# Even layer of a two-layer trunk: one sequence of weight groups, heads paired by parity, output norms and masks moved

## The chip, the cores and the metric

One core of one Trainium2 chip runs the whole program. The metric is the device time of one execution in microseconds (us); lower is better. TensorE is called PE, VectorE DVE, ScalarE ACT, GpSimd POOL and SyncE SP, as in the profile.

## The reference, cut to what matters

x is 512 tokens by 1024 features, float32. Layer 0 (the even layer) is a mixer of four gated DeltaNet heads and four differential-attention heads and then a gated MLP; layer 1 (the odd layer) is a chunk-band attention of 16 heads and another MLP.

```python
h = rmsnorm(x, even_norm_mix)
dn_qkv, dn_a, dn_b, dn_gate, fq, fk, fv = split_cols(h @ even_w_in, IN0_SPLITS)
dn_qkv = silu(causal_dwconv(dn_qkv, even_dn_conv))            # 4 taps
# gated_deltanet, per head: L = I + strict(beta * k k^T * decay); solve L [u|w] = [beta v | beta k exp(g)]
#   qk = tril(q k^T * decay); scan over chunks: v_new = u - w S; o = q_dec S + qk v_new; S = S*g_last + k_dec^T v_new
o_a = rmsnorm(o_a, even_dn_norm) * silu(dn_gate)
# diff_attention, per head: softmax(q1 k1^T) - lam * softmax(q2 k2^T), rotary q and k, block-causal mask
o_b = rmsnorm(o_b, even_diff_subln) * (1.0 - lam_init)
x = x + concatenate([o_a, o_b]) @ even_w_out
x = x + conv_gated_mlp(rmsnorm(x, ffn_norm[0]), ...)
x = x + chunk_band_attention(rmsnorm(x, odd_norm_mix) @ odd_w_qkv) @ odd_w_out
x = x + conv_gated_mlp(rmsnorm(x, ffn_norm[1]), ...)
out = rmsnorm(x, final_norm)
```

## The kernel before

**Layout.** Features lie on the 128 partitions and the 512 tokens along the free axis. Every large product is made of three matmuls of 128x512 in a split format: `mm3` (L619 to L621) multiplies head by head, tail by head and head by tail, where head is a value rounded to the fast format (`mh`, `wh`) and tail the remainder (`ml`, `wl`). The prediction calls three such matmuls a **group**. Eight groups over k make one 128-feature tile in one of four accumulators `acc`.

**Weights.** They come in units through two slots. SP loads 128x2048 floats into `raw[s]`, ACT rounds them into `wh[s]` (L373, `units_split_act`), DVE subtracts (L377, `units_split_dve`) into `wl[s]`. A slot can be split again only when PE has finished both tiles of the unit in it. In the even layer slot 0 holds q and k of a DeltaNet head and slot 1 its v and gate; for an attention head slot 0 holds q and k, slot 1 only v.

**Order.** Each engine has its program written out by hand, in order; semaphores tie them. Four PSUM tensors `R0` to `R3` serve all small products in a fixed order of jobs (`BANK`). Python generators interleave: PE walks a chain of small products and takes groups from `fill` between them; ACT and DVE walk their side and take pieces from `evac` (a convolution, a split, a SiLU) at fixed places.

**DeltaNet.** `dn_pair(p, ...)` does heads 2p and 2p+1 side by side. PE: sums of squares (L658), cumulative decays (`grow`, L720), norms spread over rows (`rk`, `rq`, L740), kk, qk, two transposes, a doubling series At, A2 ... U3, three rounds T, Y, X, then u, wT, a scan over four blocks, and at its end the output norm: square on ACT, sums on PE (`oc`), root, reciprocal, diagonal matrix, spread on PE (`ro`), and two DVE products. Before pair 0 PE has done four units (64 groups) in the opening. Two groups are taken after every step: pair 0 has 64 groups, pair 1 has 24. POOL applies the masks `triu` and `C_STRICT` to the decays before DVE uses them (L520, L523), and copies the gate (L517).

**Attention.** `attention("diff", i, ...)` runs in a hardware loop for heads 0 to 2 and once for head 3. For each of 8 score tiles DVE adds the mask and negates (L1662), ACT exponentiates (L1189); after two of them DVE normalises and combines (L1672 to L1682), PE transposes (L865), ACT copies, PE multiplies by v (L880). PE takes two groups after each of 8 steps and one after the later ones; then the next head's rotary products (L826), `stack` on ACT (L1092 to L1094) and key tails on POOL (L549), and the output norm of this head follow (L658, L1717, L895, L1221, L1723). DVE evacuates the next head's q, k, v after the last score tile.

**Output projections.** The last even head and the last odd pair take groups of the projection of the first three tiles over seven of the eight inputs; `out_rest` then does the eighth input of the three tiles, and after that all eight groups of the fourth tile. The next unit follows.

Of the kernel before, what the change touches and what calls it, by code (L numbers as in the profile page):

```python
# [30 lines left out]
P = 128  # L31
S = 512
# [15 lines left out]
ALPHA = 4  # L48
LINE = 40
# [11 lines left out]
C_ID, C_ONE, C_TRIU, C_STRICT, C_M16, C_M32, C_M64, C_M128, C_PERM = range(9)  # L61
C_COS, C_SIN, C_MASK = 9 * P, 9 * P + S, 9 * P + 2 * S
C_WIDTH = 9 * P + 3 * S


def constants():
# [26 lines left out]
_DN = [("sq_c", 0), ("grow", 1), ("gcol", 0), ("rk", 0), ("kk", 0), ("rq", 0), ("qk", 1), ("ktok", 0), ("vtok", 1),  # L93
# [13 lines left out]
class Bank:  # L107
# [5 lines left out]
    def phase(self, name, jobs, times, lead=()):  # L113

        for j in lead:
            self.at[dict(jobs)[j]] += 1
        self.base[name] = (list(self.at), jobs)
        for _, b in jobs:
            self.at[b] += times
        for j in lead:  # L120
            self.at[dict(jobs)[j]] -= 1
# [12 lines left out]
BANK.phase("dn", DN_JOBS, NH // 2)  # L134
BANK.phase("diff", DIFF_JOBS, NH, lead=("rot_q", "rot_k"))
# [5 lines left out]
BANK.phase("yt", XT_JOBS, 1)  # L141

# [15 lines left out]
def build(nc, T, out):  # L158

    ctx = ExitStack()  # L160
    with ctx:
# [90 lines left out]
        own = ("gC", "sqq", "sqk", "qh", "kh", "decT", "decN", "qd", "qkD", "N", "A", "At", "A2", "A2t", "U")  # L252
        d = [{}, {}]
        for n in ("gC", "sqq", "sqk", "qh", "kh", "decT", "decN", "qd"):
            for h in (0, 1):
                d[h][n] = sb(f"dn_{n}{h}", [P, S], F32, mix)[:, :]
# [1586 lines left out]
```

## Time and profile before

| | |
|---|---|
| three runs | 1481.82 us median (1476.59 to 1482.45) |
| profiled execution | 1482.28 us, span 1480.6 us |
| PE busy | 1415.0 us, 96% |
| DVE busy | 843.7 us, 57% |
| ACT busy | 617.9 us, 42% |
| granted PE clock, mean | 0.968 |
| PE share of the chain that ended last | 88% |

A granted clock of 1.00 is 2.4 GHz and 0.50 is 1.2 GHz. The mean of a stretch between these says how much of it ran at the lower level: at 0.95, a tenth of it. As half speed costs half of that time, (1 - clock) times the length of a stretch in which PE is busy is what the lower level cost there.

The even layer's mixer lies in the first 413 us; the opening ends at 74.9 us, pair 0 at 186.4, pair 1 at 273.8, the first attention head starts at 288.3.

### The profile page before, as it was taken

What the parts mean: (1) busy time and instruction counts of PE and PEld (TensorE: products, weight loads), DVE (VectorE), ACT (ScalarE), POOL (GpSimd) and SP (SyncE); (2) the same over time, 40 slices, a digit from 0 to 9 for tenths busy, and PEclk for the clock granted to TensorE, in tenths of its full rate; (3) what the DMA queues carried; (4) which work ended last, traced back from release to release, by engine and by line L of the source; (5) the groups of instructions that cost most, each with busy time, mean ns of one, the idle gap of its engine ahead of it and who ended that gap; (6) DMA issues with size and microseconds to landing.
All of it is one profiled execution on the core that took longest, in us unless ns stands there. A gap on an engine that the chain in (4) does not pass through costs nothing.

```text
span 1480.6 us, 19860 instructions
## 1 busy us (share of the span) xinstructions
PE 1415.0 (96%) x6775; PEld 1154.3 (78%) x6775; DVE 843.7 (57%) x1235; ACT 617.9 (42%) x865; POOL 180.9 (12%) x177
## 2 busy tenths in 40 slices
PE   5979999899989999999999999999999999999996
PEld 4769888677777888888888777777778888888875
DVE  5676665566664655346555566556556654355542
ACT  4423232355533454223334566556434452233342
POOL 1040042011232100000001221112130000000011
PEclk9979979899999999999999999999999999999997
DMA  7421101011334542343323323223233323433131
GB/s 202 130 57 29 44 15 44 0 43 57 114 86 112 161 124 64 107 114 101 86 71 96 106 62 96 65 62 97 56 89 85 100 84 87 127 85 108 58 89 57
DMA packets 218641, 124.80 MB, mean 84 GB/s; under 512 B 6047, under 2 KB 215434, under 8 KB 218340
## 3 DMA queue, kind: packets, MB, share of 16 engines
q1 hardware_dynamic: 213744, 112.54, 27.0%
q0 software_dynamic: 3664, 11.58, 2.9%
q8 instruction: 29, 0.48, 0.1%
q10 hardware_dynamic: 1188, 0.08, 0.1%
q14 instruction: 16, 0.13, 0.0%
HBM read 119.94 MB, written 9.48 MB: 87 GB/s over the span
## 4 chain that ended last, share of the span: by engine, by line
PE 88%; DVE 5%; ACT 3%; issue 2%; DMA 1%; POOL 0%; DVEq 0%; ACTq 0%; SPq 0%; POOLq 0%
PE acc L619 24%; PE acc L621 23%; PE acc L620 23%; PE R L720 4%; PE R L880 4%; PE R L865 1%; PE R L848 1%; ACT wh L373 1%; PE R L658 1%; PE R L849 1%; PE R L740 1%; DVE wl L377 1%; DVE cta L1368 1%; PE R L718 1%; DMA xin<-in_x 1%
## 5 line engine op out<-in xcount | busy, mean ns | idle before, releaser
L619 PE MATMUL acc<-mh,wh 128*128 128x512 f32 x1120 | 456.0, 407 | 9.7 <-DVE ml L1321 5.4
L621 PE MATMUL acc<-mh,wl 128*128 128x512 f32 x1120 | 440.7, 393 | 0.0
L620 PE MATMUL acc<-ml,wh 128*128 128x512 f32 x1120 | 440.7, 393 | 0.0
L377 DVE TENSOR_TENSOR wl<-raw,wh 128x2048 fp32r<-128x2048 f32 x116 | 251.8, 2171 | 137.1 <-ACT wh L373 137.1
L373 ACT ACTIVATE wh<-raw 128x2048 fp32r<-128x2048 f32 x116 | 210.1, 1811 | 151.0 <-PE acc L621 149.7
L619 PEld LDWEIGHTS acc<-mh,wh 128*128 128x128 f32 x1120 | 213.0, 190 | 58.3 <-issue 11.9
L621 PEld LDWEIGHTS acc<-mh,wl 128*128 128x128 f32 x1120 | 212.5, 190 | 46.4
L620 PEld LDWEIGHTS acc<-ml,wh 128*128 128x128 f32 x1120 | 213.2, 190 | 41.5 <-issue 2.6
L494 POOL TENSOR_TENSOR ssum<-ssum,sq 128x512 f32<-128x512 f32 x32 | 52.0, 1624 | 719.9 <-ACT sq L1012 719.3
L619 PE MATMUL acc<-ah,wh 128*128 128x512 f32 x352 | 137.7, 391 | 0.4 <-DVE wl L377 0.2
L620 PE MATMUL acc<-al,wh 128*128 128x512 f32 x352 | 137.0, 389 | 0.0
L621 PE MATMUL acc<-ah,wl 128*128 128x512 f32 x352 | 137.0, 389 | 0.0
L1764 DVE SCALAR_TENSOR_TENSOR cta<-cb,pv,cta 128x512 f32<-128x512 f32 x88 | 66.2, 752 | 74.8 <-ACT cta L1260 68.4
L1189 ACT ACTIVATE pr<-ns,nm 128x128 f32<-128x128 f32 (+3 forms) x96 | 53.8, 561 | 89.5 <-DVE nm L1662 66.6
L1260 ACT ACTIVATE cta<-cb,pv 128x512 f32<-128x512 f32 x44 | 35.9, 816 | 103.8 <-DVE cb L1757 103.6
L619 PEld LDWEIGHTS acc<-ah,wh 128*128 128x128 f32 x352 | 66.0, 188 | 16.5 <-issue 2.4
L621 PEld LDWEIGHTS acc<-ah,wl 128*128 128x128 f32 x352 | 66.1, 188 | 13.9
L620 PEld LDWEIGHTS acc<-al,wh 128*128 128x128 f32 x352 | 66.1, 188 | 13.3
L1662 DVE CUSTOM_DVE_ANT_0 ns<-R,gb 128x128 f32<-128x128 f32 (+1 forms) x64 | 30.7, 489 | 66.2 <-PE R L849 66.2
L1784 DVE TENSOR_TENSOR x<-x,acc 128x512 f32 (+1 forms) x32 | 22.0, 687 | 72.6 <-PE acc L621 72.3
L880 PE MATMUL R<-pT,av 128*64 128x128 f32 (+1 forms) x400 | 60.7, 282 | 0.1
L880 PEld LDWEIGHTS R<-pT,av 128*64 128x64 f32 (+1 forms) x400 | 44.2, 147 | 15.9 <-issue 13.2
(282 smaller groups left out, 1755.9 us busy)
## 6 DMA issues: line engine op xcount, KB each, us to landing
raw<-in_ffn_w_in SPq DMA_DIRECT2D x88, 512.0 KB, 5.0
raw<-in_even_w_in SPq DMA_DIRECT2D x24, 512.0 KB, 5.2
raw<-in_ffn_w_out SPq DMA_DIRECT2D x32, 384.0 KB, 4.0
raw<-in_ffn_w_out SPq DMA_DIRECT2D x32, 320.0 KB, 3.6
raw<-in_odd_w_qkv SPq DMA_DIRECT2D x16, 512.0 KB, 4.6
rel_bias_extended<-rel_bias_rows POOLq DMA_DIRECT2D x16, 320.0 KB, 4.1
raw<-in_even_w_out SPq DMA_DIRECT2D x8, 512.0 KB, 4.7
raw<-in_odd_w_qkv SPq DMA_DIRECT2D x16, 256.0 KB, 3.1
```

The costliest lines, as they stand in the source:

```text
L373: nc.scalar.activation(wh[s][:, 0:n], raw[s][:, 0:n], ACT.Copy).then_inc(sem(f"w_head{s}"), 1)
L377: nc.vector.tensor_tensor(wl[s][:, 0:n], raw[s][:, 0:n], wh[s][:, 0:n].bitcast(F32), ALU.subtract).then_inc(sem(f"w_tail{s}"), 1)
L494: pool.tensor_tensor(ssum[:, :], ssum[:, :], sq[s][:, :], ALU.add).then_inc(sem("ssum"), 1)
L619: nc.tensor.matmul(o, ah_, bh_, start=first, stop=False)
L620: nc.tensor.matmul(o, ah_, bl_, start=False, stop=False)
L621: return nc.tensor.matmul(o, al_, bh_, start=False, stop=last)
L720: last = nc.tensor.matmul(r[:, t], lhs, triu if b is triu else b[:, t], start=True, stop=True)
L880: last = nc.tensor.matmul(dst, av[:, k, vc], pT[y % 2][:, k * P:(k + 1) * P], start=(k == 0), stop=(k == b))
L1189: A(pr[t % 2][:, 0:w], ns[t % 2][:, 0:w], ACT.Exp, bias=nm[:, t:t + 1], scale=-1.0, accum_out=rs[:, t:t + 1]).then_inc(sem("exp_" + ph), 1)
L1260: A(cta[s][:, :], cb[s][:, ALPHA - 2:ALPHA - 2 + S], ACT.Identity, bias=pv[:, bass.ds(j + (PV_CB + JF * layer), 1)], scale=pv[:, bass.ds(j ...
L1662: free(V.tensor_tensor_reduce(out=ns[t % 2][:, 0:w], in0=r[:, 0:w], in1=bias, scale=-1.0, scalar=3e38, op0=ALU.add, op1=ALU.min, accum_out ...
L1764: V.scalar_tensor_tensor(out=cta[s][:, :], in0=cb[s][:, o:o + S], scalar=pv[:, bass.ds(j + (w0 + JF * tap), 1)], in1=cta[s][:, :], op0=ALU ...
```

## The change

Four edits. (1) Weight groups of the even layer come in one sequence that PE takes from throughout: `give(fill, n)` takes n groups, `upto(fill, n)` takes until n are taken. Slot 0 holds even heads, slot 1 odd heads: q and k of head 0 and of head 1, then v and gate of head 0 and of head 1, and so on. Only the first two units (32 groups) come before pair 0. (2) The output norm of a pair is moved into the next pair (`post_sums`, `post_rows`, `post_roots`, `post_inverse`, `post_out`), that of an attention head into the next head (`diff_rows`, `diff_gain`, `diff_scale`, `diff_round`, `diff_tail`). (3) The masks of the decays are dropped; the strict triangle is in the masks of N, and POOL masks qkD afterwards. (4) The attention heads are written out instead of looped; the output projections take all four tiles as filler and `out_rest` is gone, in the odd layer too. All matrix products stay.

```diff
 # SP: units
+            for p in (0, 1):
+                for h in (0, 1):
+                    load(h, 2 * p, pair(h, w0, c + C_Q, c + C_K))
+                for h in (0, 1):
+                    load(h, 2 * p + 1, pair(h, w0, c + C_V, c + C_GATE))
...
 # PE: DeltaNet pair
                 for h in (0, 1):
                     pe.wait_ge(sem(f"sqk{h}"), p + 1)
                     token_sums(r, 0, d[h]["sqq"])
                     done(token_sums(r, NB, d[h]["sqk"]), ph, f"sq_c{h}", 0)
+                if p:
+                    post_sums(p - 1)
                 # grow, gcol
+                give(fill, 4)
+                spread(p, "rk", "sqk", "dk", p)
+                if p:
+                    post_rows(p - 1)
+                give(fill, 4)
+                step(4, "kk", "kh", "kh", ["rk"])
+                spread(p, "rq", "sqq", "dq", p)
+                give(fill, 4)
+                step(4, "qk", "kh", "qh", ["rq"])
+                step(4, "ktok", "kh", None)
+                two, one_ = (2, 1) if p == 0 else (1, 1)
+                step(two, "At", "A", None, need=[("A_E", 4 * p + 1)])
...
+                for w, e, g in (("16", "E32", (1, two, 1)), ("32", "E64", (two, 1, two)), ("64", "E128", (1, two, 1))):
...
 # PE: attention head
+            def diff_head(i, fill):
+                for t in range(12):
+                    if t < 8:
+                        score(ph, t, 0, t % 2, t // 2, i)
+                    if t == 0 and i == 0:
+                        post_rows(1)
+                    if t == 1:
+                        values(ph, 0, UNIT["diff"] + i)
+                    if t == 2 and i:
+                        diff_rows(i - 1)
+                    give(fill, 2 if t < 4 else 1)
+                    if t == 7 and i < NH - 1:
+                        rope_products(i + 1)
+                    # t = 3, 5, 7, 9: transposes; t = 4, 6, 8, 10: product with v
...
+            dn_pair(0, fill)
+            upto(fill, 68)
+            dn_pair(1, fill)
+            upto(fill, 120 + AHEAD)          # AHEAD = 8
+            post_sums(1)
+            for i in range(NH):
+                diff_head(i, fill)
+                if i < NH - 1:
+                    upto(fill, 120 + 24 * (i + 1) + AHEAD)
+                else:
+                    give(fill, 4)
+                diff_sums(i)
+            give(fill, 100)
+            diff_rows(NH - 1)
+            run(out_terms(out0, ((), (7,)), heads_wait, 1))
+            for s in (0, 1):
+                run(features(s, out0 + 1, (oh, ol)))
...
-            attention("odd", NPAIR - 1, out_terms(UNIT["out1"], range(KD - 1), KD - 1, pairs_wait))
-            out_rest(UNIT["out1"], KD - 1, pairs_wait)
+            odd_pair(NPAIR - 1, out_terms(out1, (range(KD - 1),), pairs_wait, 2))
+            run(out_terms(out1, ((), (KD - 1,)), pairs_wait, 2))
+            for s in (0, 1):
+                run(features(s, out1 + 1, (oh, ol)))
 # ACT: attention head
+                    if t < 8:
+                        read(act, ph, f"s{t}", 0)
+                        if t >= 2:
+                            act.wait_ge(sem("pn_diff"), 4 * i + t // 2)
+                        probabilities("diff", i, t, (t // 2 + 1) * P)
+                    if t == 2 and i:
+                        diff_gain(i - 1)
+                    if t == 4 and i:
+                        diff_round(i - 1)          # oh of the head before
+                    if t in (5, 6) and i in (1, 2):
+                        k = 2 * (i - 1) + t - 5
+                        A(oh[:, k, :], om[:, k, :], ACT.Copy).then_inc(sem("oc_head"), 1)
+                    # t odd: copy of the transposes
+                    if t == 8 and i < NH - 1:
+                        units_split_act(act, 0, UNIT["diff"] + i + 2)
...
 # DVE: attention head
+                for t in range(10):
+                    # mask and negate s_t; at t = 2, 4, 6, 8 normalise and combine
+                    if t == 1 and i == 0:
+                        post_out(1)
+                    if t == 2 and i:
+                        diff_scale(i - 1)
+                    if t == 4 and i:
+                        diff_tail(i - 1)           # waits for o_head from ACT
+                    if t in (5, 6) and i in (1, 2):
+                        dve.wait_ge(sem("oc_head"), k + 1)
+                        V.tensor_tensor(ol[:, k, :], om[:, k, :], oh[:, k, :].bitcast(F32), ALU.subtract)
+                    if t == 5 and i == NH - 1:
+                        rest_split_dve(dve, 0)
+                    if i < NH - 1:
+                        if t in (5, 6):
+                            rotated_evac(i + 1, t - 5)
+                        if t == 8:
+                            rope(i + 1)
+                        if t == 9:
+                            units_split_dve(dve, 0, UNIT["diff"] + i + 2)
+                # then osb, query_tails, value_evac, units_split_dve(1), reciprocal, diagonal
...
 # DVE: opening
+            first = qk_evac(0)
+            for _ in range(4): next(first, 0)      # q0, k0
+            # abT copy
+            for _ in range(2): next(first, 0)      # split of slot 0
+            # chain of small operations on a, b (as before), waiting for ab_e from ACT
+            for _ in first: pass                   # q1, k1, split of slot 1
```

## Rows read from the trace of the kernel before

**Rows 1.** The page, busy times and granted clock in 40 slices.

```profile
PE 1415.0 (96%) x6775; PEld 1154.3 (78%) x6775; DVE 843.7 (57%) x1235; ACT 617.9 (42%) x865; POOL 180.9 (12%) x177
...
PEclk9979979899999999999999999999999999999997
```

**Rows 2.** Waits of PE: for whom, total us, times, longest.

```profile
PE R L720 <- DVE dn_decT L1447: 7.6, 1, 7.6
PE R L848 <- POOL kl L549: 6.8, 4, 4.6
PE R L895 <- DVE osd L1717: 5.5, 4, 1.4
```

**Rows 3.** Stretches of the even mixer: length, busy per engine, granted clock, DMA.

```profile
74.90:86.30 11.40, 3.81 (x33) 3.72 (x31) 8.76 (x12) 5.76 (x7) 0.61 (x1) 0.63 0.37 92
86.30:186.40 100.10, 98.91 (x612) 86.77 (x612) 69.04 (x111) 26.31 (x41) 18.80 (x14) 0.96 0.15 38
186.40:199.70 13.30, 12.00 (x55) 9.97 (x55) 8.41 (x16) 7.12 (x10) 2.29 (x2) 0.66 0.16 40
199.70:273.80 74.10, 72.46 (x491) 65.04 (x492) 46.01 (x77) 17.45 (x29) 22.08 (x18) 0.95 0.09 22
273.80:288.30 14.50, 8.87 (x27) 4.59 (x26) 8.07 (x14) 5.39 (x10) 1.25 (x1) 0.69 0.00 1
288.30:319.60 31.30, 29.20 (x137) 23.21 (x137) 19.20 (x46) 17.08 (x35) 5.46 (x5) 0.93 0.11 28
319.60:350.90 31.30, 29.13 (x136) 22.62 (x136) 21.30 (x49) 18.53 (x36) 5.69 (x4) 0.95 0.19 52
350.90:382.30 31.40, 29.15 (x137) 22.60 (x137) 21.38 (x49) 18.65 (x37) 5.71 (x4) 0.94 0.24 67
382.30:413.40 31.10, 26.61 (x123) 21.09 (x123) 15.51 (x42) 16.21 (x33) 4.25 (x6) 0.88 0.31 106
413.40:423.70 10.30, 10.28 (x33) 8.32 (x34) 6.74 (x5) 4.18 (x5) 3.80 (x2) 0.72 0.17 48
```

**Rows 4.** Chain that ended last, pair 0: start, length, what.

```profile
114.06 1.78 PE R L720 x16
117.24 1.78 PE R L720 x16
```

**Rows 5.** DVE in order of time in the opening: start, length, operation.

```profile
58.60 0.18 DVE L1611 TENSOR_TENSOR abz<-R,rcol 128x32 f32<-128x32 f32 x1
...
63.74 0.69 DVE L1356 TENSOR_TENSOR cb<-acc,rstd 128x512 f32<-128x512 f32 x1
...
68.67 2.32 DVE L1368 SCALAR_TENSOR_TENSOR cta<-cb,pv,cta 128x512 f32<-128x512 f32 x3
74.69 2.29 DVE L377 TENSOR_TENSOR wl<-raw,wh 128x2048 fp32r<-128x2048 f32 x1 [3.69 <-ACT wh L373]
...
86.24 0.42 DVE L1447 COPY dn_decT<-gall 128x512 f32<-128x512 f32 x1
```

**Rows 6.** Groups of DVE and ACT, each shape apart, attention head from 319.6 us.

```profile
L377 DVE TENSOR_TENSOR wl<-raw,wh 128x2048 fp32r<-128x2048 f32 x1 | 2.3, 2283 | 0.0
L1662 DVE CUSTOM_DVE_ANT_0 ns<-R,cst 128x512 f32<-128x512 f32 x2 | 1.4, 691 | 1.6 <-PE R L849 1.5
L1682 DVE SCALAR_TENSOR_TENSOR pn<-pr,rr,pn 128x512 f32<-128x512 f32 x1 | 0.8, 752 | 0.0
L1430 DVE TENSOR_TENSOR aq<-R,cst 128x512 f32<-128x512 f32 x1 | 0.7, 691 | 0.7 <-PE R L826 0.7
...
L1189 ACT ACTIVATE pr<-ns,nm 128x512 f32<-128x512 f32 x2 | 1.4, 725 | 2.4 <-DVE pn L1682 2.4
L1204 ACT ACTIVATE oh<-om x1 | 0.6, 615 | 0.0
```

**Rows 7.** ACT and DVE in order of time behind the odd projection's eighth input.

```profile
1064.65 1.92 ACT L373 ACTIVATE wh<-raw 128x2048 fp32r<-128x2048 f32 x1 [2.56 <-PE acc L621]
...
1066.60 2.29 DVE L377 TENSOR_TENSOR wl<-raw,wh 128x2048 fp32r<-128x2048 f32 x1 [1.14 <-ACT wh L373]
```

More of the change, by code:

```diff
@@ L48 @@
 ALPHA = 4
+AHEAD = 8
 LINE = 40
@@ L133 @@
 BANK.phase("norm0", NORM_JOBS[1:], 1)
-BANK.phase("dn", DN_JOBS, NH // 2)
-BANK.phase("diff", DIFF_JOBS, NH, lead=("rot_q", "rot_k"))
+for _p in (0, 1):
+    BANK.phase(f"dn{_p}", DN_JOBS[_p], 1)
+BANK.phase("dn2", DN_POST, 1)
+BANK.phase("rope", ROPE_JOBS, 1)
+for _i in range(NH):
+    BANK.phase(f"diff{_i}", [j for j in DIFF_JOBS if (_i or j[0] != "ro") and (_i < NH - 1 or j not in ROPE_JOBS)], 1)
+BANK.phase(f"diff{NH}", DIFF_POST, 1)
 BANK.phase("norm1", NORM_JOBS, 1)
@@ L540, in _ @@
                             .then_inc(sem(f"A_E{h}"), 1)
+                for h in (0, 1):
+                    e = d[h]
+                    read(pool, ph, f"qk{h}", 0)
+                    pool.tensor_tensor(blk(e["qkD"]), blk(e["qkD"]), rows(triu), ALU.mult).then_inc(sem(f"qkD{h}"), 1)
             def key_tails(n):
@@ L857, in attention @@
-                    run(fill, 2 if t < 8 else 1)
-                    z = (t - 3) // 2 if diff and (t - 3) % 2 == 0 else t - 2 if not diff else -1
-                    if 0 <= z < per:
-                        b = z if diff else items[z][1]
-                        pe.wait_ge(sem("pn_" + ph), per * i + z + 1)
-                        r = job(ph, f"t{z}", i)
-                        for k in range(b + 1):
-                            last = nc.tensor.transpose(r[:, k * P:(k + 1) * P], pn[z % 2][:, k * P:(k + 1) * P], ident)
-                        done(last, ph, f"t{z}", i)
@@ L1144, in dn_pair @@
-                next(evac, 0)
+                copy_out("At", "At")
+                copy_out("A2", "A2", 1)
+                copy_out("A4", "A4", 2)
+                copy_out("A8", "A8")
+                copy_out("T16", "T", 0 if p else 1)
+                copy_out("T32", "T", 0 if p else 2)
+                copy_out("T64", "T")
+                copy_out("wT", "wT", 1 if p else 3)
+                if p:
+                    stack("diff", 0)
                 for h in (0, 1):
-                    r = full(act, "dn", f"o{h}", p)
-                    A(d[h]["sqo"], r[:, :], ACT.Square).then_inc(sem(f"sqo_dn{h}"), 1)
+                    read(act, ph, f"o{h}", 0)
+                    A(d[h]["sqo"], d[h]["os"], ACT.Square).then_inc(sem(f"sqo_dn{h}"), 1)
@@ L1159, in _ @@
+            first = qk_evac(0)
+            for _ in range(3):
+                next(first, 0)
             act.wait_ge(sem("ab_in"), 1)
@@ L1441, in beta, with dn_pair, piece @@
+            def dn_pair(p, evac, pieces):
+                ph = f"dn{p}"
                 def beta(h):
                     return ball[:, 2 * p + h, :]
+                def piece(at):
+                    for _ in range(pieces.get(at, 0)):
+                        next(evac, 0)
                 for h in (0, 1):
@@ L1646, in attention @@
                 for t in range(8 + 2):
-                    if t == 9 and diff and more:
-                        next(evac, 0)
-                        rope(i + 1)
                     if t < 8:
@@ L1794, in mlp @@
                         x_tiles(3, g0 + 3, False)
-            with dve.Fori(0, NH - 1) as i:
-                attention("diff", i, NH, 0, att_evac("diff", i + 1, i + (UNIT["diff"] + 1)))
-            rest_split_dve(dve, 0)
-            attention("diff", NH - 1, NH, 0, iter(()), more=False)
+            for i in range(NH):
+                diff_head(i)
+            diff_scale(NH - 1)
+            diff_tail(NH - 1)
             out_proj(UNIT["out0"], 1)
```

1011 lines of the change are left out of this document (514 added, 497 removed), and 7 rows, old and new, of the table _DN.

## The prediction, before the changed kernel ran

> **What bounds the kernel now.** I read the page first: PE is busy 96% of the span [rows 1]. Every product stays in the change, so the time can move only by PE's idle time and by the time PE spends at the lower clock. The slices show the clock below full in the first third only, in the even mixer. The waits name three holes there [rows 2]: 7.6 us before pair 0, 6.8 us for key tails (4.6 of it before attention head 0), 5.5 us for the output norm of the four heads. Third view: the mixer in stretches [rows 3]. In each I add idle time (length minus PE busy) and clock loss, (1 - clock) x length:
>
> - opening's end, 74.9: 11.4 us long; the sums in it are about 3.6 us at full clock, so 7.8 us are lost
> - pair 0: 1.2 + 4.0 = 5.2
> - end of pair 0, 186.4: 1.3 + 4.5 = 5.8
> - pair 1: 1.6 + 3.7 = 5.3
> - end of pair 1, 273.8: 5.6 + 4.5, less what overlaps; the work in it is 5.4 us at full clock (three pieces of 1.8), so 9.1
> - four attention heads: 2.1, 2.2, 2.3, 4.5 idle and 2.2, 1.6, 1.9, 3.7 clock: 20.5
>
> That is some 54 us, 3.6% of the span, all that this change can win. Where the clock falls is plain: in stretches that are full of matmuls it is 0.93 to 0.96, in those with one-column sums and waits 0.63 to 0.72 [rows 3].
>
> **The change part by part.** The sum is made against the profiled execution, 1482.3 us (span 1480.6, 1.7 us around it); the median of the three runs is 0.5 us lower.
>
> A step of the DeltaNet chain is 1.78 us for both heads, and from step to step 3.18 us with two groups between [rows 4]; so a group is 0.70 us.
>
> *Opening, +2.2.* Pair 0 now starts after 32 groups, at 53.0 us instead of 74.9 (22 us of groups earlier). But its sums need k of head 1, and on DVE that convolution now stands behind the small chain on a and b, which takes 63.74 - 58.60 = 5.14 us [rows 5]. Its input comes from PE at about 47.6, so q1 starts at 52.7. A convolution is 3.6 us, two end at 60.0. From the end of such a convolution (68.67 + 2.32 = 71.0) through the squares, ACT's split and DVE's split it was 6.0 us (74.69 + 2.29) [rows 5], then 0.6 for the copies that release `grow`: 66.6. PE waits or sums from 53.0 to 66.6, 13.6 us against 11.4. The clock after it is taken as before. Bounds: -1 if the small chain hides under the tile, +5 if ACT's table changes fall on the path.
>
> *Pair 0, +0.8.* 68 groups instead of 64, which is only work moved in; four of them stand at each early step, one or two later. POOL's four masks of the decays and two gate copies go and two masks of qkD come, all before their users are due; PE waited for none of them [rows 2], so I count nothing. One new place: ACT does k's SiLU, two squares and a split before the T64 copy, 0.8 us late. Bounds 0 to +3.
>
> *Pair 0 to pair 1, 0.* The output norm no longer holds PE, but the first sums of pair 1 need the convolution of k3, which DVE does only after the last scan block: 3.6 us, SiLU and squares 1.9, ACT's split 1.9, DVE's split 2.3, copies 0.6. That is 10.3 us after the last scan operand, and PE has 5.4 us of sums and one group in it. It was 5.8 lost; it is 5 to 7. Bounds -3 to +3.
>
> *Pair 1, -2.7.* It has 52 groups instead of 24, so the steps that stood bare are covered; DVE's two evacuations of 0.7 and a piece of up to 1.95 us fit in 2.5 us per step on average. What stays is the clock after the sums. Bounds -4 to +2.
>
> *Pair 1 to head 0, -4.2.* Eight groups (5.6 us) cover rope, `stack` (six ACT copies, 3.6) and the square. But `post_rows(1)` stands right after the first score, while DVE must do a split and wait for a root before the diagonal: about 2.1 us idle, 0.3 before, and 2.5 of clock. 4.9 instead of 9.1. Bounds -7 to 0.
>
> *Heads.* This is the dear place. A head is 27.3 us of PE work (31.3 less 2.1 and 1.9). PE now takes one group, not two, after scores 4 to 7, has 8 groups after the head, and these need slot 0's split, which DVE does at t = 9, behind `rope` (four operations of 0.69, 2.8 us) [rows 6]. DVE and ACT are in order and hand to each other. For heads 1 and 2, from score 4 (8.6 us into the head): negate 0.64; combine 1.25; exponential 0.8 and rounding 0.6 on ACT, for which `diff_tail` waits; tail 0.69; negate 0.64; exponential 0.8 and `oh` copy 0.62, for which `ol` waits; `ol` 0.69; rotated q 0.68; negate 0.77; combine 1.5; exponential 0.75 and `oh` 0.62; `ol` 0.69; rotated k 0.68; negate 0.77; exponential 0.8; combine 1.6; rope 2.8; split 2.28. The widest forms are in [rows 6] (0.691, 0.752, 0.725, 0.615, 2.283), the narrower ones are from the same view. Sum 20.7 us. PE's own work from score 4 to those 8 groups is 12.3 us (four scores 2.3, eight groups 5.6, rotary products 1.8, transposes and products with v 2.6). So PE waits 8.4 us per head, in three or four places: before the product with v of block 1, before the rotary product of k, before the 8 groups. With an estimated 1.2 of clock that is 9.6 each, against 3.8 and 4.2: +11.2. Head 0 has neither `diff_tail` nor `ol`: 2.2 before the 8 groups and 0.8 of clock, against 4.3: -1.3. Head 3 has no rope but the tail and the rest split: PE waits 3.7; its final chain (square, root, diagonal, spread, scale, round, tail) stays bare, 4.5 idle and 3.0 clock; 11.2 against 8.2: +3.0. Together **+12.9**. Bounds -8 (DVE keeps up, no clock lost) to +24 (clock low through them). I take the sum, as it is made of measured durations in the order of the code.
>
> *Loop written out, 0.* The heads' instructions are issued once instead of from a loop; no row shows PE waiting for instructions in either form. Bounds -2 (registers at the loop's ends) to +3. SP's loads are as many and as large, and no PE wait here is for a load.
>
> *Projections, +7.2.* `out_rest` did eight groups (5.6 us) of the fourth tile behind slot 0's last input, and they covered slot 0's next split. Now only two groups follow. ACT's split starts after slot 0's last matmul, DVE's ends 68.89 - 64.65 = 4.24 us later [rows 7]. PE has 1.4 us: 2.9 idle, 0.8 clock, +3.7 in the odd layer, in which nothing else changes. In the even layer the clock is at 0.72 there [rows 3], the two groups take longer, so 2.0 idle and 1.5 clock, +3.5. Bounds +4 to +11.
>
> Sum: 2.2 + 0.8 + 0 - 2.7 - 4.2 + 12.9 + 0 + 7.2 = +16.2. 1482.3 + 16.2 = 1498.5; against the median, **1498 us**.
>
> The Trainium skill ("TensorE: Matmul & The Clock Gate", section "A second HAM failure mode: psum-queue depth-cycling") says that frequent short idles between groups of matmuls can make the clock swing between its two levels, so that the loss is more than the idles. By it, heads 1 and 2 and the pair with thinner filler would run partly at 1.2 GHz. That is the rival "low clock" below; the rows so far show it only around the sums and the long waits.
>
> **The rivals.** *Low clock, 1510.* If the waits inside heads 1 to 3 hold the clock at 0.75 over 90 us, as 0.63 to 0.72 stand in the short stretches [rows 3], that costs up to 22 us where I have 3.5, half of it inside waits: +12. Against: pair 1 with bare steps stayed at 0.95.
>
> *DVE keeps up, 1481.* DVE is busy 57% [rows 1] and 21.3 of 31.3 us in a head [rows 3]. If ACT's copies come before they are needed, heads 1 to 3 wait 2.3 each before the 8 groups. Heads 1 and 2: 6.2 against 8.0, -1.8; head 0 -1.3; head 3 nothing: -3.1 in place of +12.9, so 1482.
>
> *Faster, 1465.* One mechanism: the 8 groups ahead also outlast the split, because DVE reaches `rope` by PE's time, and PE never stops long enough to lose its clock in head 0 to 3. Then the 12.3 us of heads 0 to 2 go, the end of pair 1 gives 9, pair 1 gives 3, the projections cost 5 and the opening 2: -17. It decides by whether `wl` of slot 0 is written before PE has done the product with v of block 3. For it: all three holes of [rows 2] are addressed. Against: the sum of 20.7.
>
> *The norm isn't off the path.* If `diff_rows` still waits for the diagonal as L895 does, 1.4 to 1.5 us per head [rows 2], three heads keep 4.3 us more: 1503.
>
> **How the numbers follow.** Forecast 0.50 (own range 1489 to 1507); low clock 0.10; keeps up 0.17; faster 0.20; the norm 0.03. Within 0.5% of 1481.8 (1474.4 to 1489.2) is no change that a measurement tells. Slower: nearly all of forecast, low clock and norm, and little of keeps up, 0.59; same 0.20; faster 0.21. The range 1466 to 1511 leaves out one in ten on either side.
>
> **What would show it.** Right: in each of heads 1 and 2, PE waits over 5 us in total, on ACT's copy of transposes, DVE's rotated k, and `wl`; a head lasts about 36 us; a wait of 2 to 3 us on `wl` behind both projections; `grow` of pair 0 at 66 to 67 us. Wrong: heads of 28 to 30 us, or no wait on `wl` at about 1065 us plus the shift.

## The result, and the profile after

| | before | after |
|---|---|---|
| median of 12 runs, us (lowest to highest) | 1481.1 (1475.9 to 1482.5) | 1486.4 (1484.0 to 1489.7) |
| profiled execution, us | 1482.3 | 1484.7 |
| its span, us; mean granted clock | 1480.6; 0.968 | 1482.9; 0.972 |

After to before is 1.0042 (95% interval 1.003 to 1.0054). The change costs 6.2 us by that ratio, 5.3 by the medians and 2.4 between the two profiled executions, by which the stages below are compared. 16 were forecast. The profiled execution of the kernel before is 1.2 us above its median and that of the changed kernel 1.7 below, so the stages show the change some 3 us kinder than the medians; no profile says in which stage.

The page of the changed kernel, busy times and granted clock, against [rows 1]:

```profile
PE 1407.8 (95%) x6775; PEld 1149.7 (78%) x6775; DVE 857.3 (58%) x1251; ACT 615.3 (41%) x864; POOL 176.4 (12%) x169
...
PEclk9899899998989999999999999999999999999998
```

PE has as many matmuls. The low slices are still in the first third (and the last slice): four in both, at 8 now, where three stood at 7. PE's waits, against [rows 2] (for whom, total us, times, longest):

```profile
...
PE R L660 <- ACT dn_sqk L1142: 9.3, 2, 7.3
PE R L857 <- DVE nm L1776: 7.4, 3, 4.1
PE acc L621 <- DVE wl L384: 5.5, 4, 3.0
...
PE R L920 <- ACT pT L1279: 5.3, 3, 2.5
```

Of the three rows of [rows 2] the key tails are gone; of the diagonals of the attention heads' output norms only the last head's is left (1.3 us), and of the wait before `grow` 1.0 us. In their place stand the waits that the forecast named: for the squares before pair 0, for a rotary product behind a DVE step (L857), for ACT's copy of transposes (L920) and for the second step's weights (L621).

The stretches, against [rows 3]: opening's end, pair 0, its end, pair 1, its end, heads 0 to 3, projection:

```profile
52.90:66.30 13.40, 5.15 (x31) 4.98 (x30) 9.34 (x16) 6.66 (x9) 0.00 (x0) 0.65 0.00 1
66.30:165.30 99.00, 97.98 (x622) 86.85 (x622) 70.26 (x112) 25.39 (x38) 18.04 (x12) 0.98 0.17 43
165.30:176.70 11.40, 9.36 (x53) 9.14 (x52) 8.71 (x18) 6.59 (x10) 0.00 (x0) 0.69 0.12 29
176.70:267.90 91.20, 91.20 (x583) 80.48 (x584) 62.54 (x98) 22.28 (x34) 21.61 (x16) 0.96 0.08 21
267.90:275.70 7.80, 7.80 (x45) 6.67 (x44) 5.59 (x9) 6.05 (x10) 3.36 (x2) 1.00 0.52 132
275.70:310.20 34.50, 30.53 (x140) 22.31 (x139) 25.26 (x53) 18.17 (x35) 6.19 (x4) 0.95 0.18 47
310.20:346.70 36.50, 29.86 (x138) 22.82 (x137) 23.82 (x50) 19.03 (x37) 5.13 (x4) 0.91 0.16 44
346.70:382.10 35.40, 30.08 (x138) 23.04 (x137) 23.76 (x50) 19.03 (x37) 7.91 (x9) 0.90 0.26 68
382.10:413.65 31.55, 24.07 (x125) 18.55 (x125) 14.71 (x42) 14.10 (x31) 0.00 (x0) 0.97 0.26 91
413.65:425.90 12.25, 10.42 (x27) 7.77 (x28) 8.75 (x8) 6.79 (x8) 3.79 (x2) 0.65 0.31 85
```

PE shows as busy for all of pair 1, yet pair 1 isn't free of losses: ends of matmuls are modelled, so a short wait between two of them hides in the busy time. A better measure of a stage is its length less its PE work at the full clock, the work counted by the distances of matmuls that wait for nothing (0.227 us for one of a group's three, 0.11 for a 128-column one of a DeltaNet step). The rest is lost, to waits or the clock. By it, in us:

| stage | lost before | lost after | difference | forecast |
|---|---|---|---|---|
| opening's end | 8.2 | 10.3 | +2.2 | +2.2 |
| pair 0 | 7.3 | 3.6 | -3.8 | +0.8 |
| end of pair 0 | 5.5 | 5.5 | -0.1 | 0 |
| pair 1 | 8.8 | 3.1 | -5.7 | -2.7 |
| end of pair 1 and head 0 | 14.0 | 7.7 | -6.3 | -5.5 |
| heads 1 and 2 | 10.8 | 20.0 | +9.2 | +11.2 |
| head 3 | 9.0 | 9.1 | +0.2 | +3.0 |
| even projection | 2.8 | 6.2 | +3.4 | +3.5 |
| odd projection | 0.7 | 3.4 | +2.7 | +3.7 |
| start of the last MLP | 3.2 | 5.7 | +2.5 | 0 |
| program's end | 18.8 | 16.3 | -2.5 | 0 |
| all between (430 to 1060, 1110 to 1440 us) | 33.7 | 34.4 | +0.7 | 0 |

The rows add up to +2.5 as rounded; the profiled spans differ by 2.3. The start of the last MLP and the program's end, for which nothing was forecast, cancel each other.

Head 1 shows the chain that the forecast summed. Three answers, in order of time: PE, then DVE, then ACT (start, length, what, idle before):

```profile
324.56 0.71 PE L920 MATMUL R<-pT,av 128*128 128x128 f32 x4 [2.45 <-ACT pT L1279]
331.55 1.19 PE L857 MATMUL R<-qr,cst 128*128 128x512 f32 x1 [4.14 <-DVE nm L1776]
```

```profile
321.81 0.69 DVE L1843 TENSOR_TENSOR ol<-osb,oh 128x512 fp32r<-128x512 f32 x1 [1.36 <-ACT oh L1299]
...
324.27 0.69 DVE L1816 TENSOR_TENSOR ol<-om,oh 128x512 fp32r<-128x512 f32 x1 [1.29 <-ACT oh L1271]
...
329.50 0.69 DVE L1816 TENSOR_TENSOR ol<-om,oh 128x512 fp32r<-128x512 f32 x1 [1.46 <-ACT oh L1271]
330.11 0.68 DVE L1506 SCALAR_TENSOR_TENSOR qr<-acc,rstd 128x512 f32<-128x512 f32 x1
330.71 0.68 DVE L1776 CUSTOM_DVE_ANT_0 ns<-R,cst 128x512 f32<-128x512 f32 x1
```

```profile
323.01 0.61 ACT L1250 ACTIVATE pr<-ns,nm 128x384 f32<-128x384 f32 x1 [1.23 <-DVE nm L1776]
...
323.62 0.61 ACT L1271 ACTIVATE oh<-om 128x512 fp32r<-128x512 f32 x1
324.14 0.36 ACT L1279 ACTIVATE pT<-R 128x256 f32<-128x256 f32 x1
...
328.14 0.72 ACT L1250 ACTIVATE pr<-ns,nm 128x512 f32<-128x512 f32 x1 [3.64 <-DVE pn L1806]
```

Three times DVE idles 1.3 to 1.5 us for a rounding on ACT (`oh`) that stands behind an exponential, which waited for DVE. PE's second rotary product (`rot_k`) waits for what comes last in this line: it goes into the PSUM tensor that holds score 7 (`R1`), and DVE reads that score at 330.71, behind the third `ol` and `qr`. Hence the releaser `nm`, that is L1776, and not `qr`.

### The profile page after: what moved, and what is told of

Read it like the earlier page. It is cut to its first block, busy times and chain, and to the rows that moved or that the text cites. A ratio compares the mean times of both kernels' runs of the same rounds, so it can differ in the third digit from the quotient of the medians.

```text
span 1482.9 us, 19623 instructions
## 1 busy us (share of the span) xinstructions
PE 1407.8 (95%) x6775; PEld 1149.7 (78%) x6775; DVE 857.3 (58%) x1251; ACT 615.3 (41%) x864; POOL 176.4 (12%) x169
## 4 chain that ended last, share of the span: by engine, by line
PE 87%; DVE 6%; ACT 3%; issue 2%; DMA 1%; SPq 0%; ACTq 0%; DVEq 0%; POOL 0%; POOLq 0%
PE acc L621 24%; PE acc L623 23%; PE acc L622 23%; PE R L754 5%; PE R L950 3%; PE R L882 1%; PE R L868 1%; PE R L660 1%; DVE wl L384 1%; ACT wh L380 1%; PE R L869 1%; PE R L742 1%; PE R L752 1%; DMA xin<-in_x 1%; DVE cta L1462 1%
## 5 line engine op out<-in xcount | busy, mean ns | idle before, releaser
L621 PE MATMUL acc<-mh,wh 128*128 128x512 f32 x1120 | 458.7, 410 | 10.3 <-DVE ml L1412 5.4
L384 DVE TENSOR_TENSOR wl<-raw,wh 128x2048 fp32r<-128x2048 f32 (+1 forms) x108 | 233.5, 2162 | 118.1 <-ACT wh L380 118.0
L621 PEld LDWEIGHTS acc<-mh,wh 128*128 128x128 f32 x1120 | 213.1, 190 | 58.8 <-issue 12.2
L621 PE MATMUL acc<-ah,wh 128*128 128x512 f32 x352 | 137.7, 391 | 0.4 <-DVE wl L384 0.2
L621 PEld LDWEIGHTS acc<-ah,wh 128*128 128x128 f32 x352 | 66.0, 188 | 16.5 <-issue 2.4
L623 PEld LDWEIGHTS acc<-ah,wl 128*128 128x128 f32 x352 | 66.1, 188 | 13.9
L1776 DVE CUSTOM_DVE_ANT_0 ns<-R,gb 128x128 f32<-128x128 f32 (+1 forms) x64 | 30.7, 489 | 65.3 <-PE R L869 65.3
L621 PE MATMUL acc<-oh,wh 128*128 128x512 f32 x128 | 53.7, 419 | 10.5 <-DVE wl L384 4.8
L1357 ACT ACTIVATE ah<-pd 128x512 f32 x44 | 27.8, 632 | 69.7 <-DVE pd L1922 69.7
```

The lines of the kernel that those rows point to most:

```text
L384: nc.vector.tensor_tensor(wl[s][:, 0:n], raw[s][:, 0:n], wh[s][:, 0:n].bitcast(F32), ALU.subtract).then_inc(sem(f"w_tail{s}"), 1)
L621: nc.tensor.matmul(o, ah_, bh_, start=first, stop=False)
L623: return nc.tensor.matmul(o, al_, bh_, start=False, stop=last)
L1776: free(V.tensor_tensor_reduce(out=ns[t % 2][:, 0:w], in0=R[t % 2][:, 0:w], in1=bias, scale=-1.0, scalar=3e38, op0=ALU.add, op1=ALU.min, ac ...
```

## The experiments

Each ran beside the kernel before, and its ratio is to that kernel; edits are to the changed kernel except in `masks_only`. Most ratios rest on twelve executions of the experiment; `combo` has four, `combo_rows` five, `bare_pair1` six and `open_order` seven. Each has one profile. Waits that the expectations quote are from issue to issue, 0.1 to 0.2 us more than the view of waits shows.

**masks_only.** The kernel before with edit (3) alone.

```diff
-    put(C_M16, row // 16 == col // 16)
+    put(C_M16, (row // 16 == col // 16) & (col < row))
...
-                    pool.tensor_tensor(blk(d[h]["decT"]), blk(d[h]["decT"]), rows(triu), ALU.mult)
...
+                    pool.tensor_tensor(blk(e["qkD"]), blk(e["qkD"]), rows(triu), ALU.mult)
```

> The kernel before, with only the edit of the masks: GpSimd no longer multiplies the decays by the triangle ahead of the inverse; the lower triangle is folded into the masks of N, and qk times decay is masked behind them. Theory (GpSimd's masks of the decays were waited for by nobody for long): pair 0 and pair 1 keep their lengths within 0.7 us each, ratio 0.999 to 1.0. Rival (the masks stood on the path into the inverse, and their leaving it explains part of the 3.2 us and 5.5 us by which the pairs got better): each pair shorter by 1.5 us or more, ratio 0.998 or less.

Measured: ratio 0.9998 (0.9985 to 1.0011). Pair 0 and pair 1, against [rows 3]:

```profile
86.30:186.70 100.40, 99.00 (x612) 86.80 (x612) 68.91 (x111) 26.75 (x42) 15.97 (x12) 0.96 0.15 37
199.30:274.20 74.90, 73.04 (x494) 65.31 (x494) 45.34 (x77) 17.98 (x30) 19.53 (x16) 0.95 0.09 22
```

POOL is 2.5 to 2.8 us less busy in each. The bounds of these windows are not quite those of [rows 3]; from `grow` to the pair's output norm, pair 0 is 0.2 us shorter and pair 1 0.1 us longer than before. So that edit is worth nothing by itself, as the forecast had it. (The 3.2 and 5.5 us in the expectation are a first reading of the pairs' gains; the table above has 3.8 and 5.7.)

**bare_pair1.** The filler of pair 1 away from the steps of the inverse.

```diff
-                step(4, "ktok", "kh", None)
-
-                two, one_ = (2, 1) if p == 0 else (1, 1)
+                step(22 if p else 4, "ktok", "kh", None)
+
+                two, one_ = (2, 1) if p == 0 else (0, 0)
...
-                for w, e, g in (("16", "E32", (1, two, 1)), ("32", "E64", (two, 1, two)), ("64", "E128", (1, two, 1))):
+                for w, e, g in (("16", "E32", (one_, two, one_)), ("32", "E64", (two, one_, two)), ("64", "E128", (one_, two, one_))):
...
+                two = two or 1
```

> The changed kernel, with the filler of pair 1 taken in bulk: 22 groups of matmuls run behind the transposes of k, and none between the 18 steps of the inverse (from At to X64), which in the changed kernel have one group each. Everything else, and the sum of groups, is as it is. My prediction priced the filler's gain in pair 1 at 2.7 us, that is the one wait over 0.2 us that was seen per step; the traces show 5.5 us between the two kernels. Theory (the group also hides the short waits, below 0.2 us, that each bare step has for ScalarE's or VectorE's copy of the step before): pair 1 grows by 5 us or more, and its length, 91.2 us, to over 96; each bare step starts a full copy (0.6 us or more) late, so that 18 steps could cost up to 11 us; ratio 1.008 to 1.012. Rival (the gain of pair 1 came from the bulk of groups ahead, or from the masks that left VectorE's queue): pair 1 grows by 3 us or less, ratio under 1.006.

Measured: ratio 1.0058 (1.0038 to 1.0078). Pair 0, then pair 1:

```profile
66.80:167.40 100.60, 99.64 (x622) 88.21 (x622) 70.19 (x111) 25.35 (x38) 18.05 (x12) 0.96 0.16 43
178.90:273.70 94.80, 93.92 (x583) 81.45 (x583) 58.94 (x98) 22.61 (x34) 20.71 (x16) 0.95 0.07 20
```

Pair 1 took 94.8 us in place of 91.0 (taken, here and in the table, between the matmuls that open the stages, up to 0.2 us from the windows' bounds): 3.8, between theory (5 or more) and rival (3 or less); the ratio, under 1.006, is the rival's. Of the 3.8 us 1.5 are waits over 0.2 us (from issue to issue), 1.0 the clock, the rest (1.3) short waits. And pair 0, whose code is the same, took 1.7 us more, all clock (0.96 for 0.98): a pair's length differs by that much from one profile to another. This profile is also the slowest of its six executions, so the 1.0 us of clock may be no work of the edit. The group beside each step is then worth 2.8 us in waits, and 3.8 with the clock: about what the forecast gave it, and not the 11 that fully bare steps could cost. The remaining 1.9 to 2.9 of pair 1's 5.7 this run leaves unexplained.

**heads_ol.** Two roundings of DeltaNet outputs to the front of heads 1 and 2, on ACT and on DVE.

```diff
-                    if t in (5, 6) and i in (1, 2):
-                        k = 2 * (i - 1) + t - 5
+                    if t in (1, 2) and i in (1, 2):
+                        k = 2 * (i - 1) + t - 1
```

> The changed kernel, with one step moved: the two roundings of a DeltaNet head's output (ScalarE's copy and VectorE's difference, two of each in attention heads 1 and 2) stand at scores 1 and 2 of the head and no longer at scores 5 and 6. Theory (after score 4 ScalarE and VectorE take turns on one chain, up to VectorE's split at the head's end; PE waits for that chain): two ScalarE copies of 0.63 us and two VectorE differences of 0.6 to 0.7 us leave the chain. Heads 1 and 2 fall by about 2.5 us each, from 36.5 and 35.4 us to about 34 and 33, and the wait of 4.29 us at 326.8 us to under 2.5; time -5 us, ratio 1.001. Rival A (VectorE's total work in the head is the limit, wherever its steps stand): under 1 us each, ratio 1.004. Rival B (TensorE's low clock sets these heads): no change either, and the granted clock of the two windows stays at 0.91.

Measured: ratio 0.9996 (0.9985 to 1.0007), 6.8 us less than the changed kernel; all that it had lost. Heads 0 to 3:

```profile
275.00:309.50 34.50, 30.54 (x141) 22.39 (x140) 25.25 (x53) 18.13 (x35) 6.20 (x4) 0.95 0.18 47
309.50:341.00 31.50, 27.82 (x139) 21.02 (x138) 23.42 (x50) 19.16 (x37) 6.20 (x4) 1.00 0.18 51
341.00:372.50 31.50, 27.84 (x139) 21.02 (x138) 23.40 (x50) 19.15 (x37) 8.88 (x9) 1.00 0.29 76
372.50:406.00 33.50, 26.46 (x123) 19.88 (x123) 14.75 (x42) 14.33 (x31) 0.00 (x0) 0.87 0.25 86
```

Head 1 fell by 5.0 us, head 2 by 3.9: the chain theory holds, rival A falls, and the size was too small by half, for a reason that the column of the granted clock shows (the third from the end): it went from 0.91 to 1.00. Of head 1's 5.0 us, 2.6 are waits (from issue to issue), as expected; the other 2.4 are clock that had fallen behind them. So rival B was half right: the clock did cost, but it wasn't a cause of its own. That is no accident of one profile: in all five profiles in which both roundings stand late, heads 1 and 2 take 36.5 and 35.4 us (to 0.2), and in all four in which both stand early, the clock is 1.00 in both heads. Head 3 gave 2.0 us back (31.5 to 33.5, clock 0.97 to 0.87) with its code unchanged.

**ol_one.** Only the first of the two moves (`if t in (1, 6)`).

> Half of heads_ol: in heads 1 and 2 only the first of the two roundings moves, from score 5 to score 1; the second stays at score 6. heads_ol took 5.0 us from head 1, of it 2.6 us of TensorE's waits and 6.8 us at the low clock, which at half speed are 2.4 us more. It leaves open whether the clock's part goes in step with the waits, or at once. Theory (the clock falls behind the long wait of 4.29 us, which one rounding less shortens by 1.3 us to about 3.0, like head 2's wait of 2.97 in the changed kernel, behind which the clock fell as well): heads 1 and 2 keep a low clock of 6.8 us each and shorten by about 1.3 us each, to 35.2 and 34.1; ratio 1.002. Rival (a wait of 3 us is short enough): the low clock goes with half of the move, both heads take 32 to 33 us, ratio 1.000.

Measured: ratio 1.0025 (1.0011 to 1.0039). Heads 1 and 2:

```profile
314.80:348.40 33.60, 28.97 (x138) 22.31 (x138) 23.65 (x50) 19.03 (x37) 5.13 (x4) 0.95 0.18 48
348.40:382.00 33.60, 28.94 (x139) 22.59 (x138) 23.63 (x50) 19.03 (x37) 7.83 (x9) 0.95 0.28 74
```

Both at 33.6, neither theory's 35.2 nor wholly the rival's. In head 1 the longest wait went from 4.1 to 2.8 us and the clock from 0.91 to 0.95: its part shrinks by degrees, here in step with the waits. The heads gained 4.7 us, but the ratio moved by only 2.5: in this profile, the slowest of its twelve executions, pair 0 is 1.7 us longer than in the changed kernel and head 0 1.0 us, with the same code and a lower clock.

**heads_both.** `heads_ol`, and ACT's rounding of the head before from score 4 to behind the transposes' copy at score 3.

```diff
-                    if t == 4 and i:
-                        diff_round(i - 1)
...
+                    if t == 3 and i:
+                        diff_round(i - 1)
```

> The kernel of heads_ol (the roundings of the DeltaNet outputs at scores 1 and 2 of heads 1 and 2), with one more step moved: ScalarE rounds the attention head before (the copy to oh) behind its copy of the first transposes at score 3, no longer behind the exponential of score 4. Theory (the chain of ScalarE and VectorE from score 4 on): in heads_ol VectorE waits 1.36 us for that copy of 0.62 us before it can subtract score 5's bias, so heads 1, 2 and 3 fall by 0.6 to 1.3 us each and the time by 2 to 4 us against heads_ol, to a ratio of 0.997 to 0.998. Rival (TensorE's waits of 0.86 and 1.87 us for the copies of the transposed probabilities are what these heads wait for now, and the copy now stands just ahead of them): no gain, 0.9996 or worse.

Measured: ratio 0.9978 (0.9964 to 0.9992). Heads 1 and 2:

```profile
311.20:341.20 30.00, 27.78 (x137) 20.95 (x138) 23.34 (x50) 19.15 (x37) 6.19 (x4) 1.00 0.20 53
341.20:371.30 30.10, 27.86 (x139) 21.01 (x138) 23.33 (x50) 19.15 (x37) 8.89 (x9) 1.00 0.31 80
```

They had 31.5 us each in `heads_ol`: 1.4 to 1.5 less, a little more than the 0.6 to 1.3 that the chain theory gave, while the total fell by 2.7 us, inside its 2 to 4.

**odd_hold.** The odd projection's fourth tile: five of its seven early inputs held back.

```diff
+                        if (s, t) == (1, 1):
+                            heads = [k for k in heads if k not in held]
+                            if n == len(parts) - 1:
+                                heads = list(late) + heads
...
+            odd_pair(NPAIR - 1, out_terms(out1, (range(KD - 1),), pairs_wait, 2, held=(2, 3, 4, 5, 6)))
+            run(out_terms(out1, ((), (KD - 1,)), pairs_wait, 2, late=(2, 3, 4, 5, 6)))
```

> The changed kernel, with the groups of the odd projection's second step put otherwise: of its fourth tile only the parts of heads 0 and 1 run beside the last pair of heads, those of heads 2 to 6 follow after the eighth head. So seven groups of matmuls (4.9 us), not two (1.4 us), lie between the end of the first step and the matmul that needs the split of the weights that this end sets free. Theory (that split, 4.2 us on ScalarE and VectorE one behind the other, is what TensorE waits for): the wait of 3.14 us at 1069 us is gone, and the time falls by 3 us, to a ratio of 1.002 against the kernel before; by 6 us (1.000) if the low clock at 1101 us hangs on that wait. Rival (the wait only moves, since the first five groups now sit in the chain of the last pair of heads less): the pair takes up to 3 us longer, time unchanged at 1.004.

Measured: ratio 1.0031 (1.0018 to 1.0045). PE at the second step, first in the changed kernel, then in this one:

```profile
1072.52 0.50 PE L621 MATMUL acc<-oh,wh 128*128 128x512 f32 x1 [2.97 <-DVE wl L384]
```

```profile
1067.26 0.39 PE L623 MATMUL acc<-oh,wl 128*128 128x512 f32 x1
1067.49 0.39 PE L621 MATMUL acc<-oh,wh 128*128 128x512 f32 x1
```

The wait of 2.97 us is gone, and matmuls follow each other by 0.23 us; behind it the kernel's lead on the changed one is 3.3 us larger than ahead of it. The total shows 1.6 us, which the two intervals leave anywhere from -1 to 4. The low clock at the start of the last MLP stayed (0.77 over 15 us, where before has 1.00), so it doesn't hang on that wait. That stretch in the changed kernel, then in the kernel before:

```profile
1095.00:1110.00 15.00, 12.31 (x45) 9.48 (x44) 6.93 (x6) 5.40 (x7) 4.29 (x3) 0.77 0.25 70
```

```profile
1093.00:1108.00 15.00, 12.29 (x55) 9.18 (x55) 8.28 (x8) 5.43 (x8) 4.30 (x3) 1.00 0.25 70
```

PE waits there twice for the same DVE step, 2.0 us at the longest, in both kernels. Nine of the ten profiles with the changed projections have this low stretch in full and neither of the two with the old ones has it; why the clock falls behind these waits in the one and not in the other stays open.

**both_hold.** The same in the even projection (3 to 6 held).

> odd_hold, with the even projection held in the same way: of its fourth tile only heads 0 to 2 run ahead, 3 to 6 follow the eighth head, so that TensorE has six groups (4.2 us) and no longer two beside the split of the second step's weights. My price of the even projection was 3.5 us (the wait and nothing else); the trace of the changed kernel shows a wait of 1.94 us at 418.5 us and a low clock there. Theory (the wait goes, and the four groups that are taken from head 3 were in its waits' cover only in part): 1.5 to 3 us less than odd_hold, a ratio of 1.001 to 1.002. Rival (the groups held were hiding head 3's last chain, whose waits of 1.43 and 3.14 us grow by as much): no change against odd_hold, 1.003.

Measured: ratio 0.9998 (0.9984 to 1.0012), 4.9 us less than `odd_hold`, more than expected. Of that 1.8 lie at the start of the last MLP, where the clock over 15 us is 0.89 and not 0.77; no run shows this to be the edit's work. Head 3 and what follows:

```profile
383.30:413.70 30.40, 22.02 (x113) 16.21 (x112) 14.74 (x42) 14.10 (x31) 0.00 (x0) 0.93 0.28 94
413.70:426.00 12.30, 12.15 (x46) 9.64 (x47) 8.82 (x8) 6.96 (x8) 3.81 (x2) 0.88 0.31 84
```

The wait for `wl` went from 1.8 to 0.2 us and the clock behind it from 0.65 to 0.88: 46 matmuls begin in the second stretch, 27 in the changed kernel. Head 3, with four groups (2.7 us) fewer, is only 1.1 us shorter (30.4 for 31.55). Of the 1.6 us that came back 0.9 are waits in the view of waits (a new one of 0.7 for ACT's square, and 1.5 for 1.3 at the diagonal); the rest goes with the lower clock (0.93 for 0.97). The rival is right in kind and outweighed.

**open_order.** DVE's convolutions of head 1 around the small chain: q's ahead of it, k's between its halves.

```diff
-            for _ in range(2):
+            for _ in range(4):
                 next(first, 0)
...
+            for _ in range(2):
+                next(first, 0)
             dve.wait_ge(sem("ab_e"), 5)
```

> The changed kernel, with VectorE's order in the opening turned: q's convolution of head 1 stands ahead of the small chain on a and b, and k's convolution between the two halves of that chain; the rest as it is. Theory (grow of pair 0 waits for VectorE's convolutions of head 1, which stand behind a chain of 5.1 us, three of them idle): pair 0 starts at about 63.2 us and not at 66.4, time -3 us, ratio 1.002. Rival (the same chain then ends later and holds ScalarE's table changes, so that the squares come no sooner): pair 0 starts at 65.5 us or later, ratio 1.004.

Measured: ratio 1.003 (1.0017 to 1.0043). PE from the first sums to `grow`, in the changed kernel and in this one:

```profile
52.64 0.95 PE L660 MATMUL R<-cst,dn_sqq 128*128 128x1 f32 x8
...
61.76 1.87 PE L660 MATMUL R<-cst,dn_sqq 128*128 128x1 f32 x8 [7.29 <-ACT dn_sqk L1142]
...
66.37 1.01 PE L754 MATMUL R<-cst,dn_decT 128*128 128x128 f32 x3 [1.03 <-DVE dn_decT L1578]
```

```profile
54.92 0.95 PE L660 MATMUL R<-cst,dn_sqq 128*128 128x1 f32 x8
...
60.64 1.87 PE L660 MATMUL R<-cst,dn_sqq 128*128 128x1 f32 x8 [3.89 <-ACT dn_sqk L1142]
...
65.31 2.07 PE L754 MATMUL R<-cst,dn_decT 128*128 128x128 f32 x8 [1.09 <-DVE dn_decT L1578]
```

From first sum to `grow` it is 10.4 us where it was 13.7: 3.3 less, as the theory has it. By the clock of the trace `grow` is at 65.3, since this run reached its first sum 2.3 us later. In the seven profiles whose opening is that of the changed kernel the sum stands between 51.3 and 53.8 us, and here PE's first matmul itself was 1.1 us late, so a bound on an absolute time was a poor test; the distance between two marks is the good one. That the turned order itself delays the first sum isn't excluded: `combo` and `combo_rows`, which have it, reach it at 53.7 and 51.9. The total (1.7 us less) is inside the intervals.

**combo.** `heads_both`, `both_hold` and `open_order` together.

> The edits of heads_both, both_hold and open_order together. Theory (each wait is paid by itself): the gains add up, 6.6 us for the first move in the heads, 2 to 4 for the second, 1.6 for the odd projection, 1.5 to 3 for the even one, 3 for the opening: 1471 to 1474 us on the median before of 1479.8, a ratio of 0.994 to 0.996, faster than either kernel. Rival (TensorE's low clock takes back part, since it comes behind the first wait that is left wherever that stands): the ratio stays at 0.998 or above.

Measured: 1464.6 us against 1480.6, ratio 0.9905 (0.9886 to 0.9924): 20.3 us less than the changed kernel, where the expected ratios meant 12 to 15. The three edits by themselves measured 9.5, 6.5 and 1.8, in sum 17.8, from which 20.3 is not clear by the intervals. Heads 1 and 2 take 30.1 us each, and from 403 us on the clock stays full up to the start of the last MLP, where the changed kernel had low stretches at 422 and 453 us. The rival isn't borne out: the clock took nothing back.

**combo_rows.** `combo`, and the spread of the last pair's norm one score later.

```diff
-                    if t == 0 and i == 0:
+                    if t == 1 and i == 0:
                         post_rows(1)
```

> The kernel combo, with the spread of the last pair's output norms moved in head 0 from behind score 0 to behind score 1, ahead of the transposes of v; the rest as it is. TensorE waits 1.90 us there for VectorE's diagonal, and then 1.25 us for the PSUM tile of the transposes, which VectorE frees late. Theory (score 1 and its operands are ready, so they cover part of the first wait): head 0 falls from 34.5 to 33.5 us or less, time -1 us, ratio 0.990. Rival (the second wait grows by what the first loses, since VectorE's evacuation follows from the diagonal and the norm it sends): head 0 unchanged, 34.5 us, ratio 0.9905. Should the clock fall no longer in head 0, 1.7 us come on top.

Measured: 1456.2 us against 1479.0, ratio 0.9844 (0.9823 to 0.9865), the fastest of all. The two waits of head 0 in the changed kernel, then head 0 in `combo`, then here:

```profile
PE R L742 <- DVE dn_A L1550: 1.7, 1, 1.7
PE R L876 <- DVE dn_A L1559: 1.1, 1, 1.1
```

```profile
273.60:308.10 34.50, 30.50 (x141) 22.40 (x140) 25.23 (x53) 18.13 (x35) 6.19 (x4) 0.95 0.18 47
```

```profile
271.40:301.60 30.20, 28.92 (x140) 21.28 (x140) 25.18 (x53) 17.98 (x35) 6.19 (x4) 1.00 0.21 53
```

One line moved by one score took 4.3 us off, where the theory had 1, and 2.7 with the clock. Both waits went, 2.6 us from issue to issue, and with them 1.7 us of clock ((1 - 0.95) x 34.5). Head 0 accounts for 4.3 us. The ratio moved by 9, on four and five executions; between the two profiles it is 5.6, of which 2.2 is a head 0 that starts earlier behind the same code, and behind head 0 the kernel is 0.9 us slower.

## Why the prediction was wrong

The sign came out, and so did the mechanisms in the opening, the attention heads and the projections; the size was 10 us too large by the ratio. The measured 1486 us lies below the forecast's own range (1489 to 1507), in the band that the prediction called "no change" and gave 0.20. The step that failed is the price of the two pairs. By the steps:

- *Opening, +2.2*: measured +2.2, `grow` at 66.37 for 66.6. `open_order` shows the cause named, DVE's convolution behind the small chain.
- *Pair 0, +0.8*: measured -3.8. **This term and the next failed.** I took the clock behind the sums "as before" and saw no wait worth removing. The waits over 0.2 us fell by 0.9 us (six became three), the clock's part by 2.2 (0.96 to 0.98, [rows 3]); 1.7 of that is what the clock does by itself from profile to profile: `bare_pair1` has it back with the same code, and of ten profiles with this pair 0 seven take 99.3 to 99.7 us from `grow` to the next sums and three 100.8 to 101.3. The masks had no part.
- *Pair 1, -2.7*: measured -5.7. I priced idle time and left the busy time alone; but a chain without filler also loses short waits between matmuls that the busy time swallows. `bare_pair1` puts 2.8 on the filler, 1.3 of it such short waits, and 1.0 more with the clock; 1.9 to 2.9 of the 5.7 it doesn't show, and their cause stays open.
- *Pair 1 to head 0 and head 0, -5.5*: measured -6.3. The wait at `post_rows(1)` is there (1.7 for 2.1 us).
- *Heads 1 and 2, +11.2*: measured +9.2; 36.5 and 35.4 us for "about 36". Right in kind: `heads_ol` and `heads_both` take links out of the chain and get their time back. The split between waits and clock was off. The forecast had 8.4 of waits and 1.2 of clock per head; head 1 had 6.5 of waits (rotary product 4.1, transposes 2.4) and 3.3 of clock ((1 - 0.91) x 36.5, a part of it inside the waits). The wait before the 8 groups didn't come in head 1: the split was done in time.
- *Head 3, +3.0*: measured +0.2. The final chain stays bare (3.0 us for `ol`, 1.3 for the diagonal), and the rest split holds PE for 2.8 us, where 3.7 stood in the sum; but the clock took 0.9 us ((1 - 0.97) x 31.55) and not the 3.0 that I gave it. That was luck in part: in `heads_ol` the same head has 0.87.
- *Projections, +7.2*: measured +3.4 and +2.7. `odd_hold` and `both_hold` take the waits away by giving back the cover that `out_rest` had been; the extra clock that I put beside the odd one (0.8) wasn't lost in the changed kernel's profile. (The sum's idle 2.9 is 4.24 less 1.4, that is 2.8.)
- *Masks and the loop, 0*: masks shown; the loop not tried.

So of 13.9 us between forecast and profile, 7.6 lie in the two pairs, 2.8 in head 3, 2.0 in heads 1 and 2, 1.1 in the projections, and the small rest in the end of pair 1 and head 0 (0.8 less than forecast) and the stages between (0.7 more). In pair 0 and head 3 it is in good part the clock: I took its loss over from the stage as it was before, and it moved by 2 us either way, with the waits and without them.

The rival "low clock" (0.75 through the heads) did not come: 0.90 to 0.97. The section "A second HAM failure mode: psum-queue depth-cycling" of the Trainium skill's "TensorE: Matmul & The Clock Gate" says of another kernel that its clock swings under frequent short idles. Here head 1 of `combo_rows` has waits of 0.7 to 0.9 us (issue to issue) in three places and stays at 1.00. In head 1 the clock followed the longest wait: 4.1 us with 0.91, 2.8 with 0.95 (`ol_one`), 1.7 with 1.00 (`heads_ol`). But 1.7 us went with 0.95 in head 0, 2.8 with 0.90 in head 2 of the changed kernel, and the same wait can cost clock in one execution and not in another: at the odd projection's second step it is 2.97 us both in the changed kernel and in `ol_one`, and the clock of the 10 us around it is 1.00 in the first and 0.83 in the second:

```profile
1069.00:1079.00 10.00, 7.03 (x32) 5.49 (x31) 8.86 (x7) 7.46 (x10) 4.66 (x3) 1.00 0.40 107
```

```profile
1068.00:1078.00 10.00, 7.03 (x24) 5.30 (x23) 8.97 (x6) 7.44 (x10) 4.80 (x3) 0.83 0.38 105
```

So the length of a wait alone doesn't tell its price in clock.

## What to carry to other kernels

A bare chain costs more than its idle time: compare a stage's length with the work in it, since short waits hide in the busy time of a pipelined engine. Where two in-order engines hand to each other, work that is due late (here the roundings) belongs where neither is waited for; moved ahead of the chain it cost nothing that shows here, inside it each link costs two handovers. Waits of TensorE may cost nearly double by the clock (head 1: 2.6 us and 2.4 more), or nothing more (the 2.8 us in head 3 of the changed kernel): give the clock a range of its own, and don't take a stage's clock over from before.

## What was not expected of the hardware

- The clock's loss behind waits was nearly as large as the waits': head 1, 2.6 us of waits and 2.4 of clock removed by one move; head 0, 2.6 and 1.7, the 4.3 us that one line took off.
- The same wait of 2.97 us, at the odd projection's second step, went with a clock of 1.00 over 10 us in one profile and of 0.83 in another.
- The same two waits of PE at the start of the last MLP (2.0 and 0.7 us) were followed by a clock of 0.77 over 15 us in the changed kernel and of 1.00 in the one before; the cause stays open.
- The same code (pair 0) took 99.3 to 99.7 us in seven profiles and 100.8 to 101.3 in three, by the granted clock alone, 0.98 and 0.96 to 0.97.
